# Hybrid attention, convolution and MLP block on one core: the sums of the MLP's input move from VectorE to GpSimd, and two groups of them move down ScalarE's and VectorE's lists

## What is computed

```python
def sq_relu_mlp(h, w_up, w_down):
    return jnp.square(jax.nn.relu(h @ w_up)) @ w_down
...
        x = x + rmsnorm_2(m, g[1])
        f = sq_relu_mlp(rmsnorm_2(x, g[2]), w_mlp_up[i], w_mlp_down[i])
        x = x + rmsnorm_2(f, g[3])
```

## Time and profile before

| | |
|---|---|
| Three runs | 1716.74, 1716.88, 1715.66 us (median 1716.74) |
| Profiled execution | 1716.07 us, span 1714.3 us |
| TensorE busy | 1689.9 us of the span, 9375 matmuls |
| VectorE busy | 1272.0 us (74%) |
| ScalarE busy | 957.0 us (56%) |
| GpSimd busy | 169.7 us (10%) |
| Mean granted TensorE clock | 0.996 of full |

### The profile page before, as it was taken

One profiled execution on the slowest core, in us unless ns is written; L12 is line 12 of the kernel. 1 busy time (PEld: TensorE's weight loads), 2 busy tenths in 40 slices (PEclk: granted clock), 3 DMA queues, 4 the chain that ended last, 5 costly groups with the idle time before them and its releaser, 6 DMA issues.

```text
span 1714.3 us, 25289 instructions
## 1 busy us (share of the span) xinstructions
PE 1689.9 (99%) x9375; PEld 1460.7 (85%) x9375; DVE 1272.0 (74%) x2020; ACT 957.0 (56%) x1645; POOL 169.7 (10%) x147
## 2 busy tenths in 40 slices
PE   9999999999999999999999999999999999999998
PEld 7888877888788897789899998878887889999977
DVE  6378877776567777588698996785566968898966
ACT  4267875665426666477546464642235766464655
POOL 2011212000300000220000002420003000000041
PEclk9999999999999999999999999999999999999999
DMA  8222124214242222243232443313323432323621
GB/s 274 81 72 74 43 75 100 72 50 147 74 112 75 74 75 80 74 172 121 77 123 77 147 162 121 111 56 111 104 88 103 157 108 99 99 99 99 233 75 50
DMA packets 152786, 177.52 MB, mean 104 GB/s; under 512 B 18281, under 2 KB 126342, under 8 KB 150886
## 3 DMA queue, kind: packets, MB, share of 16 engines
q1 hardware_dynamic: 150790, 159.22, 29.4%
q10 hardware_dynamic: 1888, 16.85, 2.5%
HBM read 158.82 MB, written 12.58 MB: 100 GB/s over the span
## 4 chain that ended last, share of the span: by engine, by line
PE 93%; DVE 4%; ACT 2%; issue 1%; DVEq 0%; ACTq 0%
PE bank L1158 28%; PE bank L1159 28%; PE bank L1160 28%; PE bank L1507 2%; PE bank L1531 1%; PE bank L1426 1%; DVE split_weights L2671 1%; PE bank L1415 1%; DVE act_a L2673 0%; PE bank L1823 0%; ACT act_a L1920 0%; DVE work L2706 0%; PE bank L1341 0%; DVE act_b L2671 0%; PE bank L1325 0%
## 5 line engine op out<-in xcount | busy, mean ns | idle before, releaser
L1158 PE MATMUL bank<-act_a,split_weights 128*128 128x512 f32 (+1 forms) x1360 | 525.3, 386 | 6.3 <-DVE act_a L2671 2.0
L1160 PE MATMUL bank<-act_a,split_weights 128*128 128x512 f32 (+1 forms) x1360 | 518.7, 381 | 0.0
L1159 PE MATMUL bank<-act_a,split_weights 128*128 128x512 f32 (+1 forms) x1360 | 518.2, 381 | 0.0
L1158 PEld LDWEIGHTS bank<-act_a,split_weights 128*128 128x128 f32 x1360 | 255.9, 188 | 58.5 <-issue 6.1
L1160 PEld LDWEIGHTS bank<-act_a,split_weights 128*128 128x128 f32 x1360 | 255.7, 188 | 50.1
L1159 PEld LDWEIGHTS bank<-act_a,split_weights 128*128 128x128 f32 x1360 | 256.0, 188 | 45.2 <-issue 0.2
L1158 PE MATMUL bank<-act_b,split_weights 128*128 128x256 f32 (+1 forms) x648 | 208.3, 321 | 4.1 <-ACT work L2391 4.0
L1160 PE MATMUL bank<-act_b,split_weights 128*128 128x256 f32 (+1 forms) x648 | 207.1, 320 | 0.0
L1159 PE MATMUL bank<-act_b,split_weights 128*128 128x256 f32 (+1 forms) x648 | 207.0, 319 | 0.0
L2613 DVE TENSOR_TENSOR split_weights<-raw_weights,split_weights 128x2048 fp32r<-128x2048 f32 x55 | 127.1, 2310 | 76.2 <-ACT split_weights L1865 63.2
L1865 ACT ACTIVATE split_weights<-raw_weights 128x2048 fp32r<-128x2048 f32 x51 | 97.3, 1908 | 119.5 <-PE bank L1160 119.5
(11 more groups left out here) (356 smaller groups left out, 3259.2 us busy)
## 6 DMA issues: line engine op xcount, KB each, us to landing
raw_weights<-in_w_mlp_up SPq DMA_DIRECT2D x32, 1024.0 KB, 5.4
raw_weights<-in_w_mlp_down SPq DMA_DIRECT2D x32, 1024.0 KB, 5.3
raw_weights<-in_w_in SPq DMA_DIRECT2D x18, 1024.0 KB, 5.2
raw_weights<-in_w_conv_in SPq DMA_DIRECT2D x12, 1024.0 KB, 5.1
raw_weights<-in_w_attn_in SPq DMA_DIRECT2D x16, 512.0 KB, 5.2
raw_weights<-in_w_ple_gate SPq DMA_DIRECT2D x8, 1024.0 KB, 5.0
raw_weights<-in_w_out SPq DMA_DIRECT2D x4, 1024.0 KB, 5.2
raw_weights<-in_w_attn_in SPq DMA_DIRECT2D x4, 1024.0 KB, 5.4
```

Of the source, the lines that this page charges most:

```text
L1158: nc.tensor.matmul(dst, w[0], a[0], start=first, stop=False)
L1159: nc.tensor.matmul(dst, w[0], a[1], start=False, stop=False)
L1160: mm = nc.tensor.matmul(dst, w[1], a[0], start=False, stop=last)
```

## The change

The four sums of a group (step Q) are made by GpSimd with the same operations and shapes, and step Q is gone from VectorE's string. GpSimd waits for X of the group, and from group 1 on for VectorE's three low parts of the group before. And the strings are rearranged: X2, H2, X3 and H3 come later in both.

```diff
         ACT_MLP = ("s0 b0 t0 v0 U3 s1 b1 t1 v1 p0 p1 p2 p3 s2 b2 t2 v2 X0 p4 p5 H0 p6 p7 s3 b3 p8 t3 p9 v3 X1 p10 p11 H1 p12 p13 "
-                   "X2 p14 p15 H2 a0 p16 a1 p17 X3 a2 p18 a3 p19 H3 a4 p20 a5 p21 a6 p22 p23 p24 p25 p26 "
-                   "p27 a7 n0 a8 a9 n1 a10 n2 a11 a12 a13 n3",
+                   "p14 p15 X2 a0 p16 a1 p17 H2 a2 p18 a3 p19 a4 p20 a5 p21 a6 p22 p23 X3 p24 p25 p26 "
+                   "p27 a7 n0 a8 a9 n1 a10 H3 n2 a11 a12 a13 n3",
...
-        DVE_MLP = ("T0 b0 y0 t0 v0 U3 T1 b1 y1 t1 v1 S0 p0 p1 p2 z0 p3 T2 b2 y2 t2 v2 Q0 p4 p5 H0 p6 S1 p7 T3 b3 y3 p8 t3 p9 v3 z1 "
-                   "Q1 p10 p11 H1 p12 p13 S2 Q2 p14 p15 H2 p16 z2 p17 Q3 p18 p19 H3 p20 S3 p21 p22 p23 z3 p24 p25 p26 p27 n0 n1 n2 n3",
+        DVE_MLP = ("T0 b0 y0 t0 v0 U3 T1 b1 y1 t1 v1 S0 p0 p1 p2 z0 p3 T2 b2 y2 t2 v2 p4 p5 H0 p6 S1 p7 T3 b3 y3 p8 t3 p9 v3 z1 "
+                   "p10 p11 H1 p12 p13 S2 p14 p15 p16 z2 p17 p18 H2 p19 p20 S3 p21 p22 p23 z3 p24 p25 p26 p27 n0 n1 H3 n2 n3",
...
+            def x_sums_made(layer, kp):
+                pool.wait_ge(x_sum_hi, x_sum_count(layer, kp, 5, 2))
+                if kp == 0:
+                    pool.wait_ge(stash_saved, 16 + 48 * (layer + 1))
+                else:
+                    pool.wait_ge(x_sum_ready, x_sum_count(layer, kp - 1, 7, 7))
+                (b11, b12), (b21, b22) = ([sq[:, h, TOKENS[t]] for t in range(2)] for h in range(2))
+                t1, t2, t3, t4 = (x_sum_made(f"t{i}", kp) for i in range(1, 5))
+                add = nc.gpsimd.tensor_tensor
+                add(t1, b12, b11, ALU.subtract).then_inc(x_sum_ready, 1)
+                add(t3, b22, b12, ALU.subtract).then_inc(x_sum_ready, 1)
+                pool.wait_ge(x_sum_ready, x_sum_count(layer, kp, 7, 1))
+                add(t2, b22, t1, ALU.subtract).then_inc(x_sum_ready, 1)
+                pool.wait_ge(x_sum_ready, x_sum_count(layer, kp, 7, 3))
+                add(t4, b21, t2, ALU.subtract).then_inc(x_sum_ready, 1)
+
             for layer in range(2):
                 sum_squares(KT, last=True)
                 sum_squares(KT)
+                for kp in range(KT // 2):
+                    x_sums_made(layer, kp)
                 sum_mlp_squares()
```

More of the change, by code:

```diff
@@ L3326, in up_mix @@
                         V.tensor_tensor(sq[:, 1, :], fourth[:, :], sq[:, 1, :], ALU.add).then_inc(up_mixed, 1)
[L3328 to L3339, removed]
                 def x_sums_lo(kp):
@@ L3454, in mlp @@
                             up_mix(c, k // 4, k % 4)
-                        elif what == "Q":
-                            x_sums_made(k)
                         elif what == "H":
```

## The result

The changed kernel takes 1726.37 us (median of 5, 1724.64 to 1727.20) against 1716.74: a ratio of 1.0052, 95% interval [1.0041, 1.0064]. It is 9.6 us slower where I forecast 3.7, and above the range. The profiled execution took 1727.20 us, its span is 1725.0.

The account below looks back on a forecast made before the run. TensorE, busy 99% of the span, was taken as the bound. Pauses of 4.8 us a layer against 2.9 and 3.75 gave +1.9 and +1.0, half clock +0.8: +3.7 on 1716.74, so 1720.4 us, range 1715.5 to 1723.5.

Parts of the forecast that it names:

- Turns at the port: GpSimd's sums and VectorE's two-input operations alternate at SBUF, 0.60 and 0.55 us a turn; H0 1.3, H1 3.2 late.
- H1's wait: Sign expected in the changed profile: H1 on ScalarE waits 3 us and more for GpSimd.
- p10 and p12: Layer 0's down units: TensorE pauses for these late low parts, 0.6 and 1.6 us.
- a0: Copy out of a bank in layer 0's down units, ready at 790.6: TensorE's old 2.0 us wait for it goes.
- p14 ("one turn of Q2 … 0.7"): Its low part stands behind three weight sums on VectorE and one GpSimd turn: TensorE pauses 0.7 us.
- X2 now comes behind p15 and ends at 790.1; four turns end it at 794.7: Group 2 in layer 0: GpSimd's four sums alternate with VectorE from the start; H2 then takes 1.1 us.
- a2's pause: Layer 0's down units: the copy a2 stands behind H2, done at 796.4 to 796.5, so TensorE pauses 1.8 us.
- the sum without its half-clock term: Change of pauses in the down units: +1.9 us in layer 0 and +1.0 in layer 1.
- Half clock: One stretch at 1.2 GHz expected behind pauses in one layer, costing 1.5 us unhidden; half taken, +0.8.
- upper case: Rival: the same mechanism with longer holds or a half-clock stretch in both layers, 1722.5 to 1725 us; chance 0.12.
- The hold of the whole instruction: Alternative bound: each GpSimd turn lasts 0.74 us, not 0.60; 1.7 us more a layer, 1723.8 in all.

Follow-up runs that it names:

- second profile of after: The changed kernel, unchanged, executed and profiled once more: 1725.53 us.
- break at p14: Changed kernel plus one VectorE wait: p14's low part waits for the third sum of S2, right before it; 1718.30 us, ratio 1.0012.
- sums alone: Kernel before with only the sums moved to GpSimd, its orders kept: 1728.66 us, ratio 1.0068.
- the mixes: Kernel before plus four chained, unread GpSimd 128x256 subtractions in chunk 3 of each layer, during VectorE's 14 mixes: 1716.69 us in one run.
- six offsets: Kernel before plus six unread GpSimd subtractions per layer in chunk 3, each behind a memset of another width: 1720.15 us in one run.
- X2 moved: Changed kernel with X2 one step later on ScalarE, behind the copy a0: 1724.51 us, ratio 1.0049.
- idle subtractions: Kernel before plus four chained, unread GpSimd 128x256 subtractions per group when its X is ready: 1734.08 us, ratio 1.0108.
- the memsets: Kernel before plus four GpSimd memsets of 128x256 output beside each group, in place of unread subtractions: 1716.23 us, ratio 0.9999.
- break at p14 or p15: The p15 one: changed kernel with VectorE's p15 low part waiting for p14's, the operation right before it; 1719.40 us in one run.
- the three kernels with later or VectorE's sums: Changed kernel's orders with sums on VectorE, 1710.23 us; the same with groups 2 and 3 later, 1709.53; GpSimd's sums with later groups, 1713.43.

## Why the prediction was wrong

- *Turns at the port* (Q0, Q1): right, and in size. H0 starts at 771.68 (forecast 771.6), H1 at 785.61 (785.6), the four sums of Q1 last 1.07 to 1.19 us. H1's wait is 2.26 us, where I had named 3 and more as a sign.
- *p10 and p12*: right. TensorE is 0.31 and 1.28 us idle there, and the matmul behind a pause takes 0.1 longer; I had pauses of 0.6 and 1.6, though my own times for them, 783.8 against 783.3 and 788.2 against 786.8, give 0.5 and 1.4. In layer 1 p10 has none, and in the second profile of after the passed-over sum of Q1 made p12's 1.93.
- *a0*: right, its wait is gone.
- *p14 ("one turn of Q2 … 0.7")*: didn't come, since GpSimd was passed over there. With the break at p14 it came: 0.44 idle.
- ***The step that failed: "X2 now comes behind p15 and ends at 790.1; four turns end it at 794.7".*** It took for granted that a waiting GpSimd gets in at VectorE's next instruction. The sums began at 790.25 and ended at 795.41 + 0.72 = 796.13; a2's pause became 3.59 idle where I had 1.8. The break at p14 shows that the other steps hold once this entry is right: with GpSimd let in at p14, a2's pause is 1.60 idle, the down units of layer 0 take 44.68 us where I had 44.9, and the kernel is 2.1 us slower than before, where the sum without its half-clock term said 2.9. The rows that I used for turns showed GpSimd meeting single long instructions of VectorE, never a back-to-back stream.
- *Half clock* (+0.8): the number of stretches was as forecast in one profile of after (one, in layer 1) and too low in the other (both layers). Its price was too low for the long one: layer 0 of the same kernel takes 46.12 us without one and 48.70 with one, 2.6 more, where I had 1.5; that stretch has 0.50 in three windows of 2 us. The one of the first profile is shorter (0.69, 0.50 and 0.96 in the windows from 1386 on) and costs about 1.5 by an estimate: 47.32 less 46.12 - 0.3, since without stretches layer 1 is 0.3 us shorter than layer 0 (44.41 and 44.68 with the break at p14). The down units of both layers add up to 93.4 and 95.0 us, against 86.8 before and 89.1 with the break; those last are +2.3, where my sum without its half-clock term said +2.9. What is left between +6.6 or +8.2 and the +9.6 of the medians I can't place; the pause in chunk 3 is a part of it in some executions. More time at the half clock is another: two of after's five executions, both of 1726.4 us, have a mean granted clock of 0.993, the others, the profiled one among them, 0.995, and those of before 0.995 to 0.997. Where that time lies isn't known, since they weren't profiled.
- *The range*: its upper case counted longer holds or more half clock, at most 1725. That one late entry brings both a longer pause and the stretches behind it wasn't in it.
- *The hold of the whole instruction*, 0.74 us, which the prediction took from the Trainium skill ("SBUF — State Buffer", "Who interferes with whom") and set aside: the turns measured are those of 0.60, since VectorE's operations in Q1 start 1.15 us apart, which is 0.55 + 0.60 (with holds of 0.74 it would be 1.29), and H1 came at 785.61, where four such holds would put it near 786.2. The same section of the Trainium skill says "Issue order, not op shape, decides who blocks." By that the sum of Q2, which started at 790.25, should have had the port before p14 at 790.57; the trace differs.
- *Chunk 3*: not foreseen, and not there in each execution.

Why the change loses at all, in two numbers: four sums on VectorE took 1.47 us of its full stream (787.79 to 789.26 in before's timeline), 0.37 each, and a sum on GpSimd takes 0.55 us of the same stream, whose operations start 1.15 us apart beside it (782.61 and 783.76 in after) and 0.60 apart without. The move costs VectorE more than it saves, as the prediction had it, and the result comes later besides. What stays open is why an entry is passed over at all. In the sums alone (Q2's first took 0.84 us), in the mixes and at six offsets GpSimd got in at once although VectorE had no visible gap; in Q2 of after, with X2 moved, and in the idle subtractions of group 2 it didn't. At Q1 it got in at once in 15 of the 16 places that the profiles hold, and was passed over in one, layer 1 of after's second profile. All 21 first operations of a group that were passed over, in six profiles, got in at an operation of VectorE with 0.03 or 0.10 us of idle time ahead of it. That the entry ends at VectorE's next break is shown; what begins it isn't.

## What to carry to other kernels

Price each two-input operation that goes to GpSimd beside a full VectorE by what it takes out of VectorE's stream (0.55 us here, against the 0.37 that it relieves it of), and add the case that the first one gets in only at VectorE's next break. Where someone waits for the result, a wait of VectorE for the instruction just before it is such a break: it left VectorE idle for 0.1 us here, and the kernel got back 7.5. And test order and engine apart: the order was worth 5.9 us, the engine cost 15.5, and their sum hid both. The engine's cost isn't one number either: 12.6 us with before's order, 15.5 with after's, some 4.0 with the groups behind the copies of products.

## What the runs showed that I had not expected

- A GpSimd operation that reads SBUF can be passed over by several back-to-back VectorE operations: 2.81, 2.33, 1.58 and 3.45 us for a 128x256 operation that takes 0.74 alone. At one place the same kernel took 1.10 us three times and 2.31 once.
- A `memset` of the same size on GpSimd at the same moments costs nothing (1716.23 against 1716.34).
- The half clock doesn't follow from the pause alone. Behind the 2.0 to 2.2 us idle of before's order it came in the down units of one of the two layers in each of four kernels with that pause (before, the memsets, the mixes, the offsets); with after's pauses in four layers of six (after, its second profile, X2 moved), once behind p12's pause of 1.93 us and not a2's; with the sums alone, behind 4.0 us idle, in both layers; with the idle subtractions behind two of the three pauses of each layer; with the break at p14 or p15, and in the three kernels with later or VectorE's sums, in none of ten layers.
